# w_down dealt to the partitions by pairs of rows: one run of 8 KB per partition in place of two of 4 KB

## The reference, cut to what matters

```
def expert_block(args):
    xb, e = args
    gu = xb @ w_gu[e] + b_gu[e]                  # w_gu[e]: 1024 x 2048
    gate, up = gu[:, :D_FF], gu[:, D_FF:]
    gate = jnp.minimum(gate, SWIGLU_LIMIT)
    up = jnp.clip(up, -SWIGLU_LIMIT, SWIGLU_LIMIT)
    hmid = (up + 1.0) * gate * jax.nn.sigmoid(SWIGLU_ALPHA * gate)
    return hmid @ w_down[e] + b_down[e]          # w_down[e]: 1024 x 1024
```

## Time and profile before

| | |
|---|---|
| median of three runs | 1490.38 us |
| the profiled execution: its own time / its span | 1490.47 / 1488.7 us |
| TensorE busy | 1412.6 us, 95% |
| VectorE / ScalarE / GpSimd busy | 467.1 / 200.1 / 50.4 us |
| moved by DMA | 450.90 MB, mean 303 GB/s over the span |
| w_gu: loads, KB each, us from issue to landing | 256, 1024.0, 16.4 |
| w_down: loads, KB each, us from issue to landing | 128, 1024.0, 15.4 |
| longest group: L940 | 2048 matmuls, 465.7 us |
| L965 | 1024 matmuls, 245.1 us |

### The profile page before, as it was taken

One profiled execution on the slowest core, in us unless ns is written; L12 is line 12 of the kernel. 1 busy time (PEld: TensorE's weight loads), 2 busy tenths in 40 slices (PEclk: granted clock), 3 DMA queues, 4 the chain that ended last, 5 costly groups with the idle time before them and its releaser, 6 DMA issues.

```text
span 1488.7 us, 18331 instructions
## 1 busy us (share of the span) xinstructions
PE 1412.6 (95%) x6808; PEld 655.9 (44%) x6808; DVE 467.1 (31%) x950; ACT 200.1 (13%) x311; POOL 50.4 (3%) x135
## 2 busy tenths in 40 slices
PE   3999889989979899999999999999999999999995
PEld 3777677767654433333333333333333333333331
DVE  2064542231223552223322332233223322332233
ACT  2114410041022110000000000000000000000002
POOL 2001000200001000000000000000000000000000
PEclk9999878986789899999999999999999999999998
DMA  8243120630057199999999999999999999999984
GB/s 269 76 150 113 59 65 0 227 129 1 1 152 286 75 400 416 416 419 418 418 416 418 418 419 416 418 418 418 417 417 419 419 417 416 419 419 418 416 340 169
DMA packets 103950, 450.90 MB, mean 303 GB/s; under 512 B 11665, under 2 KB 20955, under 8 KB 71046
## 3 DMA queue, kind: packets, MB, share of 16 engines
q1 hardware_dynamic: 96520, 442.91, 74.2%
q10 hardware_dynamic: 7398, 7.56, 1.9%
HBM read 444.27 MB, written 6.26 MB: 303 GB/s over the span
## 4 chain that ended last, share of the span: by engine, by line
PE 63%; DVE 1%; issue 0%; ACT 0%; DVEq 0%
PE ps L940 29%; PE ps L965 16%; PE ps L918 7%; PE ps L898 5%; PE ps L912 2%; PE ps L926 1%; PE ps L906 1%; PE ps L935 1%; PE ps L958 1%; DVE x_tok L1709 0%; DVE x_tok L1683 0%; ACT proj L1228 0%; ACT proj L1224 0%; DVE proj L1664 0%; DVE proj L1668 0%
## 5 line engine op out<-in xcount | busy, mean ns | idle before, releaser
L940 PE MATMUL ps<-ring,proj 128*64 128x512 f32 x2048 | 465.7, 597 | 0.0
L940 PEld LDWEIGHTS ps<-ring,proj 128*64 128x64 f32 x2048 | 140.8, 137 | 256.3 <-issue 247.7
L965 PE MATMUL ps<-ring,proj 128*64 128x512 f32 x1024 | 245.1, 601 | 0.9 <-ACT proj L1224 0.9
L1683 DVE TENSOR_TENSOR x_tok<-x_tok,ps 96x512 f32<-96x512 f32 x192 | 122.9, 679 | 109.8 <-PE ps L918 109.8
L1658 DVE TENSOR_SCALAR proj<-ps 128x512 f32<-128x512 f32 x32 | 22.1, 691 | 403.4 <-PE ps L940 403.4
L965 PEld LDWEIGHTS ps<-ring,proj 128*64 128x64 f32 x1024 | 65.0, 136 | 151.0 <-issue 148.8
L552 PE MATMUL ps<-feat,ring 128*128 128x288 f32 x384 | 109.8, 450 | 0.0
L918 PE MATMUL ps<-proj 64*96 64x512 f32 x384 | 105.8, 628 | 3.6 <-DVE x_tok L1683 2.8
L541 PE MATMUL ps<-feat,ring 128*128 128x288 f32 x384 | 96.4, 415 | 0.0
L552 PEld LDWEIGHTS ps<-feat,ring 128*128 128x128 f32 x384 | 80.7, 213 | 24.2
L898 PE MATMUL ps<-proj 96*64 96x512 f32 x384 | 89.9, 603 | 0.0
(11 more groups left out here) (355 smaller groups left out, 1032.1 us busy)
## 6 DMA issues: line engine op xcount, KB each, us to landing
ring<-in_w_gu SPq DMA_DIRECT2D x256, 1024.0 KB, 16.4
ring<-in_w_down SPq DMA_DIRECT2D x128, 1024.0 KB, 15.4
ring<-in_w_in SPq DMA_DIRECT2D x12, 2048.0 KB, 8.1
out<-states SPq DMA_DIRECT2D x1, 2048.0 KB, 8.7
ring<-in_w_oa SPq DMA_DIRECT2D x1, 2048.0 KB, 15.3
ring<-in_w_ob SPq DMA_DIRECT2D x1, 2048.0 KB, 7.7
ring<-in_w_out SPq DMA_DIRECT2D x1, 2048.0 KB, 7.5
out<-states ACTq DMA_DIRECT2D x1, 2048.0 KB, 8.7
```

Source lines behind the costliest of these rows:

```text
L940: last = mm(bank(j // 2)[64 * (j % 2):64 * (j % 2) + 64, :], xgT[:, k % 4, k // 4, :], ring[:, k, 512 * j:512 * j + 512], start=False, sto ...
L965: last = mm(bank(4)[64 * j:64 * j + 64, :], hidT[:, k % 4, 64 * (k // 4):64 * (k // 4) + 64], ring[:, KT + k // 2, n:n + 512], start=False ...
L1683: tt(x, x, bank(5 + j)[0:TP, :], ALU.add).then_inc(sg["comb_taken"], 1)
```

## The change

A slot of w_down still gets 256 consecutive rows, 1 MB. They are dealt otherwise: partition p now gets rows 2p and 2p + 1 of them, which lie side by side in memory, as one run of 8 KB. So half j of a slot holds the rows 2p + j, and the gated values that meet them are no longer 128 consecutive columns, but every second one of 256. `turn_hid` picks them with a column step of two. The output of each transpose has the shape that it had, and `down` is unchanged.

```
             def down_load(e, k):
                 src = w_down[0, e, 256 * k:256 * k + 256, :] if isinstance(e, int) else \
                     w_down[0][bass.ds(e, 1), 256 * k:256 * k + 256, :].rearrange("a p n -> (a p) n")
-                sp.dma_start(ring[:, KT + k, :].rearrange("p (j n) -> p j n", j=2),
-                             src.rearrange("(j p) n -> p j n", p=128)).then_inc(w_arrived[KT + k], 16)
+                sp.dma_start(ring[:, KT + k, :], src.rearrange("(p j) n -> p (j n)", j=2)).then_inc(w_arrived[KT + k], 16)
...
                 for c in range(4):
-                    last = tr(hid_T[:, c, :], hid[:, 128 * c:128 * c + 128], ident[:])
+                    last = tr(hid_T[:, c, :], hid[:, 256 * (c // 2) + c % 2:256 * (c // 2) + 255 + c % 2:2], ident[:])
                 last.then_inc(sg["hid_turned"], 1)
```

## The result

Over 20 runs each the changed kernel takes 1494.47 us in the median (1486.71 to 1496.04) and the kernel before 1488.95 (1483.86 to 1493.37). The ratio is 1.0031, with a 95% interval of 1.0020 to 1.0042: slower by 3 to 6 us (4.6 by the ratio, 5.5 by the two medians), which is less than the 0.5% that I had called no change, but clear of zero. The time lies in the range of the prediction, 4 us above its centre.

What follows compares the result with a forecast made beforehand. TensorE was taken to bound the expert stage, with transfers covered by a reserve. Transfers 0, issue 0 and turn 0 on the median of 1490.38 us gave 1490.4 us, no change; range 1486.5 to 1496.5.

Steps and rivals of the forecast that it cites:

- TensorE sets the time, the transfers live on a reserve: Expert loop: TensorE paces blocks at 29.83 us; transfers need about 30.10 and draw on lead built before the loop.
- 0.29 us per block for the transfers, none on the path: w_down loads in the expert loop: 8 KB runs cut transfers from 30.10 to 29.81 us per block, saving no kernel time.
- The step falls on the weight load: Turn of the gated values (L926): the strided tile is loaded as weights, the identity moves; one load takes 140 ns.
- Cost of the step: 0: Four transposes per block (L926): strided reading adds nothing; bounds were 0 and 17.9 us in all.
- my own formula for that case: L926, load taking p ns of port: (p - 60) plus 3 x (p - 110) per block; 2.9 us at p = 120.
- The forecast fails if a block is off 29.83 us: Sign for the changed kernel's profile: an expert-stage block other than 29.83 us would refute the forecast.
- its rule for this case: If the four L926 exceed 0.66 us, the strided load is responsible, costing that excess times 32.
- The half-rate case: L926 weight load twice as slow, p = 120: 90 ns a block, 2.9 us in all, 1493.3 us.
- The two rules of the Trainium skill: L926 loads: two reads per 16-byte line run at full rate, 1490.4 us; 107 ns per load gives 1503.8 at half rate.
- Slower rival, 1501.0 at three times: Strided weight load at L926 three times as slow, p = 180: 330 ns a block, 10.6 us in all; chance 0.08.

Runs made afterwards that it cites:

- The pairs alone: The changed kernel's w_down load (rows 2p and 2p + 1 per partition) with the old side-by-side turns, against the kernel before: 1488.58 us, ratio 1.0007.

## Why the prediction was right, and where it was not

*TensorE sets the time, the transfers live on a reserve.* Right. The pairs alone change nothing, and once TensorE had 1.3 us less per block the waits for in_w_gu appeared and the block rose to the pace of the transfers. One reading behind it was wrong: the DMA row is at nine in 24 slices, not 28. Nothing hangs on it.

*0.29 us per block for the transfers, none on the path.* Right in both: 30.12 against 29.82 measured with the transfers as the bound. I had landing stop at 13 us; it fell to 11.0, because the block itself got longer.

*The step falls on the weight load.* Right, by the 140 ns that became 209.

*Cost of the step: 0.* Wrong, and the only term that was. I wrote "I take 0: the nearest row is the contiguous load with 50 ns of slack behind each turn, and half the rate would hardly pass it". The load did go at half the rate, p = 120, and my own formula for that case gives 90 ns a block and 2.9 us, against 91 ns and 2.9 measured. By its own sign ("The forecast fails if a block is off 29.83 us") the forecast of nothing failed in the block, 29.92, and its rule for this case held: the four turns are 0.75 us, 0.09 over 0.66, times 32 is 2.9. The mistake was in the choice, not in the working: the first load of a group has no slack in front of it, so any slowdown is paid there, and taking 0 meant to assume no slowdown at all, on no row. The half-rate case was the natural one and should have been the centre, 1493.3.

*The two rules of the Trainium skill.* The one on 16-byte lines (SBUF — State Buffer, Door 1: The DMA port swizzle), which backed the 0, doesn't hold for this load. The Trainium skill's figure for a weight load (TensorE: Matmul & The Clock Gate, LDWEIGHTS), an estimate of 107 ns for 128 columns, gave 419 ns a block at half the rate; 91 were measured, and a strided load takes 120 ns of its port, a contiguous one 60.

*Slower rival, 1501.0 at three times.* Right in place, too dear: the step makes the load two times as long on its port, at two and at four.

*Not foreseen:* half-clock stretches behind the start of the last block, worth 3.4 us in two of three traces of the changed kernel and, inferred from the clock, in most of its runs. Without them the median would be near 1491, an estimate. I had not looked at what the end costs when TensorE idles there.

*Luck.* The centre stood on a median of three runs, 1490.38, and that of twenty is 1488.95, so the loss is 5.5 us and not 4. The range up to 1496.5 was made wide for a load 2.4 times slower, 6.0 us; what filled it was a load at twice and a clock that I hadn't reckoned with. That the time fell inside is in part luck.

## What to carry to other kernels

When two engines are both at nine tenths, look whether the pace changes while the other side's latency drifts: a constant block over a growing landing time says which is the bound, and the drift per block gives the other one's rate before it ever binds. A strided operand belongs on an engine with slack: the same step was 1 ns on VectorE and 91 ns a block on TensorE, where it doubled the weight load. A transfer that gets faster is worth its gain only together with an edit that makes the bound engine quicker: alone the pairs brought 0, and with 0.44 us less of TensorE per block they brought 6 us (1483.40 against 1477.34).

## What the runs showed of the hardware that was not expected

- A float32 weight load of 128 columns takes 0.12 us of its port at a column step of two and 0.06 at one; its duration is 209 ns at two, 212 at four, 141 at one.
- VectorE's multiply of 128 x 512 float32 takes 692 ns with both operands at a step of two, 691 without.
- A 96 x 128 transpose of float32 by `transpose` takes 0.40 us for three, by a matmul with the identity 0.84.
- A queue of loads in 8 KB runs moves 422 GB/s, in 4 KB runs 410, and the blocks that waited for it bear it out (29.82 and 30.12 us). Issuing a load of w_down takes SP 333 ns by pairs and 373 to 383 before.
- A granted clock at the lower level for 6.8 us in the last block (and again on its last matmuls), from within 1.83 us of idle time of TensorE on, in two of three traces of one kernel. The third has the same idle time and the full clock.
